# Moving a kernel's weight buffers by 32 bytes in every partition, with nothing else changed

## The reference

```python
# layer 0, and per group of tokens
xa, ga, q, k, v = split(rmsnorm(x) @ w_in_ab)         # 1024 -> 5 * 1024
h = recurrence(conv4(xa)); ya = h * gelu(ga)
yb = attention(rope(q), cache + rope(k), cache + v)    # three dilation groups, merged
x = x + rmsnorm(concat(ya, yb) @ w_out_ab)             # 2048 -> 1024
x = x + rmsnorm(square(relu(rmsnorm(x) @ w_up)) @ w_down)   # 1024 -> 4096 -> 1024
# layer 1
xm, z = split(rmsnorm(x) @ w_in_c)                     # 1024 -> 2 * 2048
q, k, v, gates = block_diag(silu(conv4(xm))), ...
C_new = decay * C + sum_s (k_s * w_s) outer v_s        # 8 samples x 4 heads x 512 x 512, read and written
y = ((headnorm(num / den) + skip * xc) * silu(z)) @ w_out_c
```

## The kernel before

| phase 0 | phase 32 |
|---|---|
| `ones`, `ident`, `par`, `tiny` | `w_raw`, `w_lo`, `w_hi`, `kv_a`, `kv_b`, `kv_w` |
| `xin_hi`, `xin_lo`, `hid_hi`, `hid_lo`, `relu` | `x`, `y`, `sq`, `sqsum` |
| `yb_hi`, `yb_lo`, `y1_hi`, `y1_lo` (shown as `y_hi`, `y_lo`) | `ya_hi`, `ya_lo`, `gaqkv`, `tp` |
| `hT`, `z`, `cring` slots 7 to 9 | `cring` slots 0 to 6 |

## Time and profile before

### The profile page before, as it was taken

The page is one execution under the profiler, slowest core; times in us unless marked ns, Lnnn a source line. Parts: engine busy times, 40 slices in busy tenths (PEclk is TensorE's granted clock), DMA queues, the critical chain, the costliest instruction groups (busy, mean ns, idle before and its releaser), DMA issues.

```text
span 1111.0 us, 21578 instructions
## 1 busy us (share of the span) xinstructions
PE 1057.6 (95%) x8479; PEld 917.5 (83%) x8479; DVE 653.9 (59%) x960; ACT 529.9 (48%) x862; POOL 184.2 (17%) x250
## 2 busy tenths in 40 slices
PE   5999999899999999999899999899989999999995
PEld 5988787689999999998899955453529999999995
DVE  5567584643475543336896566868794485544333
ACT  5333654533566553435565344463624456553431
POOL 5134000000114220101400430412100104220100
PEclk9999999999999999999999999999989999999998
DMA  9799898999445445443743059999998535445531
GB/s 353 249 337 344 317 331 282 384 379 409 156 133 167 158 168 168 158 167 121 273 156 122 1 185 406 351 390 358 393 386 324 171 114 171 159 162 170 162 122 43
DMA packets 92763, 261.23 MB, mean 235 GB/s; under 512 B 8934, under 2 KB 10086, under 8 KB 92410
## 3 DMA queue, kind: packets, MB, share of 16 engines
q1 hardware_dynamic: 91818, 258.69, 65.3%
q0 software_dynamic: 432, 1.29, 0.4%
q10 hardware_dynamic: 432, 0.14, 0.0%
HBM read 218.36 MB, written 41.73 MB: 234 GB/s over the span
## 4 chain that ended last, share of the span: by engine, by line
PE 80%; DVE 9%; ACT 4%; POOL 2%; issue 2%; DMA 1%; SPq 1%; DVEq 0%; POOLq 0%; ACTq 0%
PE ps L2096 21%; PE ps L2098 20%; PE ps L2097 20%; PE ps L2208 2%; PE ps L2571 2%; PE ps L2610 2%; DMA w_raw<-in_weights 1%; PE ps L2596 1%; DVE cring L1787 1%; PE ps L2289 1%; PE ps L2463 1%; PE ps L2451 1%; PE ps L2190 1%; DVE x L1328 1%; DVE w_lo L1243 1%
## 5 line engine op out<-in xcount | busy, mean ns | idle before, releaser
L1243 DVE TENSOR_TENSOR w_lo<-w_raw,w_hi 128x1024 fp32r<-128x1024 f32 x232 | 286.1, 1239 | 211.5 <-ACT w_hi L718 210.4
L718 ACT ACTIVATE w_hi<-w_raw 128x1024 fp32r<-128x1024 f32 x232 | 242.4, 1054 | 212.5 <-PE ps L2098 172.3
L2096 PE MATMUL ps<-xin_hi,w_hi 128*128 128x288 f32 x1016 | 305.5, 301 | 14.9 <-DVE w_lo L1243 14.9
L2098 PE MATMUL ps<-xin_hi,w_lo 128*128 128x288 f32 x1016 | 302.7, 298 | 0.0
L2097 PE MATMUL ps<-xin_lo,w_hi 128*128 128x288 f32 x1016 | 301.9, 297 | 0.0
L2096 PEld LDWEIGHTS ps<-xin_hi,w_hi 128*128 128x128 f32 x1016 | 192.0, 189 | 27.0 <-DVE w_lo L1243 16.6
L2097 PEld LDWEIGHTS ps<-xin_lo,w_hi 128*128 128x128 f32 x1016 | 192.1, 189 | 0.7
L2098 PEld LDWEIGHTS ps<-xin_hi,w_lo 128*128 128x128 f32 x1016 | 191.4, 188 | 0.0
L2098 PE MATMUL ps<-hid_hi,w_lo 128*128 128x288 f32 x512 | 152.6, 298 | 0.0
L2096 PE MATMUL ps<-hid_hi,w_hi 128*128 128x288 f32 x512 | 151.3, 296 | 0.0
L2097 PE MATMUL ps<-hid_lo,w_hi 128*128 128x288 f32 x512 | 151.3, 296 | 0.0
(11 more groups left out here) (414 smaller groups left out, 1659.4 us busy)
## 6 DMA issues: line engine op xcount, KB each, us to landing
w_raw<-in_weights SPq DMA_DIRECT2D x232, 512.0 KB, 3.4
cring<-in_C SPq DMA_DIRECT2D x64, 512.0 KB, 6.4
out_Cs<-cring SPq DMA_DIRECT2D x64, 512.0 KB, 7.2
kv_a<-in_kv SPq DMA_DIRECT2D x56, 448.0 KB, 6.0
kv_b<-in_kv SPq DMA_DIRECT2D x52, 448.0 KB, 6.3
kv_w<-in_kv SPq DMA_DIRECT2D x20, 448.0 KB, 7.6
out_Cp<-cring SPq DMA_DIRECT2D x8, 512.0 KB, 7.2
out_v<-gaqkv SPq DMA_DIRECT2D x1, 1152.0 KB, 14.9
```

Of the source, the lines that this page charges most:

```text
L718: act.activation(w_hi[:, l % UM], w_raw[:, l % W_SLOTS], ACT.Copy).then_inc(hi_ready, 1)
L1243: dve.tensor_tensor(w_lo[:, l % W_SLOTS], w_raw[:, l % W_SLOTS], w_hi[:, l % UM], ALU.subtract).then_inc(lo_ready, 1)
L2096: pe.matmul(out, w_hi[:, j, ws], hi, start=start and kk == 0, stop=False)
L2098: last = pe.matmul(out, w_lo[:, l % W_SLOTS, ws], hi, start=False, stop=stop and kk == UK - 1)
```

## The change

`tiny` is laid out behind the weights' parts instead of ahead of them. So the weights' parts, and all that share their bytes, begin 32 bytes earlier, with phase 0 instead of 32. `tiny` itself goes 65,536 bytes further on, and keeps phase 0. It takes the 32 bytes that were given up, so `x` and everything behind it stay where they were. Distances within the moved region are unchanged, so the tensors there keep their phases relative to each other. The two programs have the same instructions in the same order on every engine (4477 written rows for TensorE, 758 for VectorE, 721 for ScalarE, 102 for GpSimd, 297 for SyncE).

```diff
@@ -171,7 +171,6 @@
         par, o = at("par", 0, NPAR)
         ident, o = at("ident", o, P)
         ones, o = at("ones", o, P)
-        tiny, o = at("tiny", o, 2)
         w_raw_at = o
         w_raw, o = at("w_raw", o, W_SLOTS, TILE)
         w_lo, _ = at("w_lo", w_raw_at, W_SLOTS, TILE, dt=F32R)
@@ -180,6 +179,7 @@
         spare_at = o
         o = o + 4 * TILE * UM
         w_parts_end = o
+        tiny, o = at("tiny", o, 2)
         x, o = at("x", o, MT, T)
         rstd_at = o
         rstd, o = at("rstd", o, T)
```

## The result

| | before | after |
|---|---|---|
| median in the same comparison, 7 executions each | 1113.25 us (1110.18 to 1114.38) | 1107.34 us (1105.18 to 1109.56) |
| the profiled execution | 1112.83 us, span 1111.0 | 1108.32 us, span 1106.5 |

The ratio is 0.9946, with a 95% interval of 0.9934 to 0.9959: the change makes the kernel 0.54% faster, 5.9 us. The forecast was no change.

A forecast was written before the change was run, and what follows sets the result against it. The prediction took TensorE, streaming matmuls, as the main bound, with DMAs full in some stretches. TensorE, ScalarE, VectorE, GpSimd and DMA terms were all 0, leaving 1114.0 us; the 8-in-10 range was 1111.2 to 1116.8 us.

The forecast's parts named there:

- the ring's pairs: VectorE's updates in the ring: items 4 and 5 stay at 2.47 us, items 7 and 8 at 2.46.
- the DMAs' ceiling: Streaming of state C: rate stays at a ceiling of 408 GB/s whatever the slot, stage 183 us long, effect zero.
- the pairs of the earlier trace: Same kinds of instruction on tensors of both phases (first byte modulo 64) before the change, read as showing zero effect.
- TensorE's term: 5568 matmuls on `w_hi` or `w_lo`: effect taken as zero, with 2.8 us either way as an unlikely bound.
- the pair: Matmuls on `ya` (equal phase, 132.7 ns) against `yb` (unequal phase, 133.2 ns), 22 intervals each, taken as no difference.
- The collision of the two streams: TensorE rival: equal phases in 5376 matmuls cost 1 ns each, 1119.4 us; slower by collision or otherwise: chance 0.04.
- The rival of whole lines in the DMAs: State C stage shortens by 3.8 us, 1.5 us elsewhere: 1108.7 us; faster by this or an engine's operand: chance 0.07.
- the prediction's estimate: By the skill's rule, stores from ring slots 0 to 6 take 66 beats instead of 67: 1.0 us less.
- the signs that I named for being wrong: Ceiling at 412 GB/s or more with a 179 us stage, under 745 matmuls, or 1024-column instructions changing over 1%.
- the sign for being right: Between 900 and 1000 us, 750 matmuls start again, or within two of that.

The follow-up runs named there:

- the cells at difference 32: Matmuls alone, 144 per cell, nothing else running, activations starting 32 bytes after the weights modulo 128: 133.3 or 134.4 ns for a matmul.

## Why the prediction was wrong

The error lies in one term, TensorE's.

**The part that held.** Loads of weights at 188 ns, ScalarE at 1060, VectorE at 1223, the ring's pairs at 2.47 and 2.46 us, the DMAs' ceiling: every engine and queue but TensorE's matmuls does the same from phase 0 as from 32, as the pairs of the earlier trace rows said. That no instruction and no order changed holds too.

**The step that failed: TensorE's term, "so the 0.5 ns is what rounding leaves. I take zero."** It put at nothing what came out at 5.5 us. Rounding was not the mistake; these three were.

First, *the pair compared two slow cases.* I divided the starts by 64 and took `ya` for equal and `yb` for unequal phase. Modulo 128 these are the differences 0 and 32, and both are slow. The state that the change creates, 64, stood in neither. A pair answers only for the states that it holds, and the modulus was an assumption that nothing in the trace supported.

Second, *a second pace was in the trace, in a stage that I did not read.* Timeline of TensorE in before, the first matmul of a step on `y` and of the step twelve later:

```profile
844.41 0.30 PE L2096 MATMUL ps<-y_hi,w_hi 128*128 128x288 f32 x1
...
882.50 0.30 PE L2096 MATMUL ps<-y_hi,w_hi 128*128 128x288 f32 x1
```

38.09 us for 288 intervals are 132.3 ns, in a kernel whose other dense stages go at 133.3. `y_hi` starts at 64 and has difference 96 (`y_lo` 32); I had called both phase 0 and put them with `xin`. So the trace held two paces at one "phase", and 5568 matmuls at the bottleneck turn 1 ns into 5.6 us. I should have read the pace of every dense stage over hundreds of matmuls, not over 22. This would have shown that the pace is not one constant; the size and the way of the change it would not have given, since the `y` stage itself has two paces at these starts, as told under what stays open.

Third, *the price was taken from the pair and not from the paces.* I priced this term at 2.8 us, from the 0.5 ns between `ya` and `yb`. That difference was nothing: in the longest stretch on `ya` without a gap the trace of before has

```profile
268.19 0.29 PE L2096 MATMUL ps<-ya_hi,w_hi 128*128 128x288 f32 x1
...
273.79 0.29 PE L2096 MATMUL ps<-ya_hi,w_hi 128*128 128x288 f32 x1
```

which are 42 intervals in 5.60 us, 133.3 ns, the pace of `yb`. And the 750 matmuls that I took for those of `hid` are nearly all of the up projection, on `xin`, whose loads of high weights reach to 994.9 us. Nothing in these readings says what another difference of the starts would do; the bound of 2.8 us rested on two stretches in the same slow state.

The corrected term: the matmuls whose difference goes from 32 to 64 are those on `xin` (232 steps less 64 on `hid`, 16 on `y`, 8 each on `ya` and `yb`: 136, 3264 matmuls), `hid` (1536) and `yb` (192), together 4992. At 133.3 - 132.2 = 1.1 ns that is 5.5 us, and 0.7 us more for the steps of before at 134.4: 6.2 us against 5.9 measured, whose interval reaches from 4.6 to 7.3. The start, where TensorE waits for weights, can't gain all of its share. `ya` (difference 96 - 64 = 32 after, 0 before) stays slow, with its median of 296 ns where `hid` has 294. `y` is a mixture after too (0 and 64), and was fast already in the profiled execution of before.

**The rivals.** The collision of the two streams had the right place and the wrong sign: it named the relation of the operands as the only new thing at the bottleneck, priced 1 ns of the 133 at 5.4 us, and gave it to the slower side. The new relation could as well have been the better one. I gave the gain on this term no rival and no chance of its own. The rival of whole lines in the DMAs came close in time, 1108.7 us against 1107.34, by luck, since the runs don't bear its mechanism out: its stage did not shorten (182.8 and 183.6 us), the best slice has 409 GB/s and not 412, and the experiment that moves only `hid` changes the pace with the weights where they were. By the rule of the Trainium skill ("DMA: Bandwidth & Descriptors", "How a descriptor splits into AXI transactions") a slot of the ring that starts 64 instead of 96 bytes past a multiple of 256 saves one beat in 67, by the prediction's estimate 1.0 us of the stage. The traces show no sign of it, 183.6 us after and 183.0 with the weights back at their old start, under a ceiling of 409 and 408 GB/s; they do not exclude so little.

**The signs.** Of the signs that I named for being wrong none came: I had asked for fewer than 745 matmuls in 100 us and not for more than 752. What caught it was the sign for being right, "750 or within two of that": there are 756.

**What stays open.** The runs show on what the pace depends, not what makes it so. At the same starts two paces occur: the two MLPs of the kernel with only raw and low weights moved; the `y` stage, which takes 132.3 ns in before and, with the weights back at their old start, 38.40 us for the same 288 intervals, 133.3 ns, as in the two other versions that leave `y` and these weights in place (`hid` moved, activations at 112):

```profile
842.36 0.30 PE L2096 MATMUL ps<-y_hi,w_hi 128*128 128x288 f32 x1
...
880.76 0.30 PE L2096 MATMUL ps<-y_hi,w_hi 128*128 128x288 f32 x1
```

and the cells at difference 32. So something besides the starts decides among two paces, perhaps what ran before the stretch, and no run tells what.

## What to carry to other kernels

Where one engine streams for most of the span, read its pace for every stage over hundreds of instructions, and multiply a difference by the count before putting it at nothing: 1.1 ns were 5.5 us here. A difference of 0.5 ns over 22 intervals is no reading, neither of an effect nor of its absence. When two tensors are compared to judge an address, list their starts modulo several powers of two, for both operands, and check that the state after the change is among the cases compared. Moving the moving operand or the weights by 16 to 64 bytes costs nothing to try; a small program of matmuls alone finds the good pair, and the kernel has to confirm it.

## What the runs showed of the hardware

- Back-to-back matmuls of 128 x 288 in the reduced fp32 format take 131.1 to 134.4 ns each at a granted clock of 1.00, mostly 131.1, 132.2, 133.3 or 134.4, which are equal steps of 1.1 ns; some starts off the grid of 32 bytes gave values in between (131.7, 133.8). For starts at multiples of 32 bytes, and one difference for all matmuls of a stretch, the pace goes by the difference of the two operands' starts modulo 128: slow at 0 (133.3) and 32 (133.3 or 134.4), fast at 64 and 96 (132.2).
- Starts at odd multiples of 16 bytes can be faster still (131.1 ns, weights at 112 and activations at 256, in two programs and in the kernel), or vary from one program to the next (132.2 and 134.4 ns at 16 and 256, 132.2 and 131.2 at 48 and 256).
- The Trainium skill ("TensorE: Matmul & The Clock Gate", "Wait — 56ns, not 53.3ns?") gives N / 2.4 GHz and a fixed 2.5 ns for back-to-back matmuls at the full clock, which makes an estimate of 122.5 ns here. The runs show 131.1 to 134.4 for this format with a load of weights for each matmul: more, and not fixed, so the measurement decides.
- From a start of 96 modulo 128 and from one of 64, ScalarE's high part of 1024 columns took 1059 and 1060 ns, VectorE's low part 1223 and 1223, a load of weights 188 and 188, and DMAs with 2 KB runs reached 408 and 409 GB/s.
